# One tiled transformer kernel: the bias row, the causal convolution and the order of cuts around the recurrent block moved between engines

## The reference

```
u = h @ w_in + b_in ;  x_br = u[:, :1024] ;  y_br = gelu(u[:, 1024:])
xc = conv_b + sum over tap of x_br shifted by tap * conv_w[tap]      (4 taps)
r, ig = sigmoid(xc @ w_ga + b_ga), sigmoid(xc @ w_gx + b_gx)         (8 blocks of 128)
a = exp(-8 r softplus(-a_param)) ;  b = sqrt(1 - a*a) * ig * xc
hs = scan of h_t = a_t h_(t-1) + b_t ;  out = (hs * y_br) @ w_o + b_o
gla: b = cumsum of log_sigmoid(...) in chunks of 64 ; q, k scaled by exp(+-b)
```

## Time and profile before

| | us |
|---|---|
| median of 3 runs | 992.35 |
| lowest and highest | 992.27, 993.11 |
| the profiled execution: its time | 992.27 |
| the profiled execution: span from first to last instruction | 991.0 |
| VectorE busy | 680.2 |
| ScalarE busy | 583.2 |
| GpSimd busy | 73.1 |

### The profile page before, as it was taken

The page is one execution under the profiler, slowest core; times in us unless marked ns, Lnnn a source line. Parts: engine busy times, 40 slices in busy tenths (PEclk is TensorE's granted clock), DMA queues, the critical chain, the costliest instruction groups (busy, mean ns, idle before and its releaser), DMA issues.

```text
span 991.0 us, 13523 instructions
## 1 busy us (share of the span) xinstructions
PE 983.3 (99%) x5222; PEld 836.4 (84%) x5222; DVE 680.2 (69%) x1151; ACT 583.2 (59%) x1016; POOL 73.1 (7%) x84
## 2 busy tenths in 40 slices
PE   9999999999999999999999999999999999999997
PEld 6887788888888998888888888888888888888886
DVE  6877776655667888766566678778576544677564
ACT  6677755444547896645454575557675644575443
POOL 2213110000000250000000000000120001000000
PEclk9999999999999999999999999999999999999999
DMA  9753445564555445555655556455543433335551
GB/s 366 296 198 123 175 170 204 200 205 177 203 180 173 168 170 176 184 194 188 215 185 198 186 197 229 174 196 184 186 152 131 170 128 128 128 128 202 181 191 42
DMA packets 27263, 180.32 MB, mean 182 GB/s; under 512 B 3008, under 2 KB 3904, under 8 KB 6464
## 3 DMA queue, kind: packets, MB, share of 16 engines
q1 hardware_dynamic: 26336, 176.89, 50.2%
q0 software_dynamic: 288, 2.10, 0.5%
q10 hardware_dynamic: 576, 0.47, 0.2%
HBM read 178.40 MB, written 1.05 MB: 181 GB/s over the span
## 4 chain that ended last, share of the span: by engine, by line
PE 92%; DVE 5%; ACT 2%; issue 1%; ACTq 0%; DVEq 0%
PE bank L326 23%; PE bank L281 15%; PE bank L283 15%; PE bank L282 15%; PE bank L334 12%; PE bank L296 1%; DVE lo L1287 1%; ACT L L886 1%; PE bank L451 1%; DVE L L1360 1%; PE bank L568 1%; PE bank L297 1%; DVE L L1424 1%; PE bank L427 1%; PE bank L435 1%
## 5 line engine op out<-in xcount | busy, mean ns | idle before, releaser
L1287 DVE TENSOR_TENSOR lo<-raw,hi 128x1024 fp32r<-128x1024 f32 x318 | 378.7, 1237 | 19.5 <-ACT hi L801 19.5
L801 ACT ACTIVATE hi<-raw 128x1024 fp32r<-128x1024 f32 x318 | 320.2, 1050 | 87.3 <-PE bank L283 86.9
L326 PE MATMUL bank<-X,hi 128*128 128x512 f32 x1080 | 284.3, 396 | 0.0
L326 PEld LDWEIGHTS bank<-X,hi 128*128 128x128 f32 x1080 | 196.9, 189 | 34.7
L334 PEld LDWEIGHTS bank<-X,lo 128*128 128x128 f32 x1080 | 147.3, 190 | 10.8
L334 PE MATMUL bank<-X,lo 128*128 128x256 f32 x1080 | 150.6, 282 | 0.0
L832 ACT ACTIVATE bt<-bank 128x256 f32<-128x256 f32 x143 | 54.2, 380 | 153.5 <-PE bank L326 145.2
L1301 DVE TENSOR_TENSOR zr<-bank,bt 128x256 f32<-128x256 f32 x64 | 27.1, 424 | 108.9 <-ACT bt L832 108.9
L281 PE MATMUL bank<-hi,zh 128*128 128x512 f32 x256 | 100.1, 391 | 0.0
L283 PE MATMUL bank<-hi,zl 128*128 128x512 f32 x256 | 99.9, 390 | 0.0
L282 PE MATMUL bank<-lo,zh 128*128 128x512 f32 x256 | 99.7, 389 | 0.0
(11 more groups left out here) (308 smaller groups left out, 1395.8 us busy)
## 6 DMA issues: line engine op xcount, KB each, us to landing
raw<-in_w SPq DMA_DIRECT2D x64, 1024.0 KB, 4.8
raw<-in_rin SPq DMA_DIRECT2D x8, 1024.0 KB, 4.8
raw<-in_wk SPq DMA_DIRECT2D x4, 1024.0 KB, 9.8
raw<-in_wq SPq DMA_DIRECT2D x4, 1024.0 KB, 8.1
raw<-in_wo SPq DMA_DIRECT2D x4, 1024.0 KB, 4.8
raw<-in_mk SPq DMA_DIRECT2D x4, 1024.0 KB, 4.8
raw<-in_mv SPq DMA_DIRECT2D x4, 1024.0 KB, 4.8
raw<-in_rout SPq DMA_DIRECT2D x4, 1024.0 KB, 4.7
```

Of the source, the lines that this page charges most:

```text
L326: return PE.matmul(bank[b][:, :], wh[:, c:c + P], x[:, k_, :, :].rearrange("p a b -> p (a b)"), start=k_ == 0, stop=k_ == NC - 1, skip_gro ...
L801: ACTE.activation(hi[u_ % HIS][:, c], raw[u_ % RAW][:, c], ACT.Copy).then_inc(hi_cut, 1)
L1287: DVE.tensor_tensor(lo[u_ % RAW][:, c], raw[u_ % RAW][:, c], hi[u_ % HIS][:, c].bitcast(F32), ALU.subtract).then_inc(lo_cut, 1)
```

## The change

Five things are changed. The first tap of the convolution goes from ScalarE to VectorE, as a multiplication and addition of two per-partition scalars, and VectorE finishes one n before it joins the next, each step waiting for the one before. Gates 6 and 7 go behind rin 4. The addition of `bo` to `h` goes from VectorE to GpSimd, where it is one operation, ahead of the `ig` products, together with the scaling of `mk` 2 to 5. On ScalarE the high cuts of mv 1 go behind the Gelu and the copies of rin 6, and `gh` 4 and 5 ahead of those of rout 1; on VectorE scans and products are done in pairs in one call, and the low cuts of mv 1 stand behind the first pair's products. In the gv stage VectorE cuts one tile less ahead.

```diff
@@ TensorE
-        plain("rin", 4, X, (4, 5), (6, 7))
+        plain("rin", 4, X, (4, 5))
+        gates(6)
+        gates(7)
@@ ScalarE
             for n in (2 * i, 2 * i + 1):
                 second("rin", n, func=ACT.Identity, bias=gain("rec_b_in", n))
-            for n in (2 * i, 2 * i + 1):
-                a.wait_ge(*free["rin", n])
-                ACTE.activation(xc[:, n, :], xbr[:, n, 0:S], ACT.Identity, scale=gain("rec_conv_w", n),
-                                bias=gain("rec_conv_b", n)).then_inc(tap_made, 1)
...
-        at_tile("rin", 7)
         a.wait_ge(*free["rin", 11])
         ACTE.activation(yb[:, 0:4, :], yb[:, 0:4, :], ACT.Gelu_apprx_tanh).then_inc(y_made, 1)
...
         to_y(6, ACT.Gelu_apprx_tanh)
+        at_tile("rin", 7)
         gated(0)
         to_y(7, ACT.Gelu_apprx_tanh)
         at_tile("mv", 0)
         gated(2)
+        gated(4)
         at_tile("mv", 1)
         copy_tokens(mv, "mv", 0)
-        gated(4)
-        at_tile("rout", 0)
         gated(6)
-        for i in range(1, 4):
+        for i in range(4):
             at_tile("rout", i)
@@ VectorE
-                d.wait_ge(bo_added, 2)
+                d.wait_ge(bo_added, 1)
...
                 joined(xbr[:, n, 3:XW], "rin", n)
-            for w in range(1, 4):
-                for n in (2 * i, 2 * i + 1):
-                    if w == 1:
-                        d.wait_ge(tap_made, n + 1)
-                        d.wait_ge(*free["rin", n])
-                    else:
-                        d.wait_ge(v_step, steps[0] - (0 if w == 3 and n % 2 else 1))
+                d.wait_ge(*free["rin", n])
+                step(DVE.tensor_scalar(xc[:, n, :], xbr[:, n, 0:S], gain("rec_conv_w", n), gain("rec_conv_b", n), ALU.mult, ALU.add))
+                for w in range(1, 4):
+                    own()
                     x = DVE.scalar_tensor_tensor(...)
...
-        lo_to(2 * (T_OF["rin", 5] + HIS))
-        d.wait_ge(bo_in, 16)
-        for s_ in range(2):
-            DVE.tensor_tensor(h[:, s_, :], h[:, s_, :], bo[:, :], ALU.add).then_inc(bo_added, 1)
         lo_to(2 * (T_OF["rin", 6] + HIS))
...
         lo_to(2 * (T_OF["rin", 7] + 2))
-        first = recur(0)
+        recur(0)                       # scans and, now inside it, products
         lo_to(2 * (T_OF["rin", 7] + HIS))
-        gate_y(0, first)
-        gate_y(2, recur(2))
         gated_low(0)
+        recur(2)
         lo_to(2 * (T_OF["mv", 0] + HIS))
         gated_low(2)
-        gate_y(4, recur(4))
+        recur(4)
         lo_to(2 * (T_OF["mv", 1] + HIS))
         gated_low(4)
-        gate_y(6, recur(6))
-        lo_to(2 * (T_OF["rout", 0] + HIS))
+        recur(6)
         gated_low(6)
...
         for i in range(4):
-            lo_to(2 * (T_OF["gv", i] + HIS))
+            at_tile("gv", i)
             decay_sum(i)
             if i:
                 decayed(i - 1)
-        lo_to(2 * (T_OF["dz", 0] + HIS))
+        at_tile("dz", 0)
         decayed(3)
@@ GpSimd
         for j in range(2):
             by_rows(mk, "mk", j, "mem", 2, mk_scaled)
+        g.wait_ge(bo_in, 16)
+        g.wait_ge(hn_made, 4)
+        g.wait_ge(ssq_made, 8)
+        POOL.tensor_tensor(h[:, :, :], h[:, :, :], bo[:, :].unsqueeze(1).to_broadcast([P, 2, D]), ALU.add).then_inc(bo_added, 1)
+        for j in range(2, 6):
+            by_rows(mk, "mk", j, "mem", 2, mk_scaled)
         for n in range(NC):
             g.wait_ge(*free["gate", n, 1])
             POOL.tensor_tensor(ig[:, n, :], ig[:, n, :], xc[:, n, :], ALU.mult).then_inc(gi_made, 1)
-        for j in range(2, 6):
-            by_rows(mk, "mk", j, "mem", 2, mk_scaled)
```

More of the change, by code:

```diff
@@ L117, in build @@
     z_made, z_high, z_low = sem("z_made"), sem("z_high"), sem("z_low")
-    tap_made, xc_made, t_made = sem("tap_made"), sem("xc_made"), sem("t_made")
+    xc_made, t_made = sem("xc_made"), sem("t_made")
     gi_made, a_made, aa_made, mass_made, root_made, drive_made = (
@@ L299, in feature, with plain @@
             return PE.matmul(bank[b][:, :], wh[:, c:c + P], both_, start=False, stop=True, skip_group_check=True)
-        def plain(name, i, x, banks, within=()):
+        def plain(name, i, x, banks):
             t = T_OF[name, i]
@@ L308, in plain @@
                     c = k_ * 256 + j * 128
-                    if j == 1 and k_ == 4:
-                        for n in within:
-                            gates(n)
                     p.wait_ge(lo_cut, cut_at(t, k_ // 4))
@@ L1500, in to_x @@
                         step(x)
-                    else:
-                        x.then_inc(xc_made, 1)
+                x.then_inc(xc_made, 1)
         for i in range(4):
@@ L1522, in recur @@
                 step(DVE.tensor_tensor_scan(tt[:, n, :], rg[:, n, :], ig[:, n, :], 0.0, ALU.mult, ALU.add))
-            return steps[0]
-        def gate_y(n0, scanned):
             for n in (n0, n0 + 1):
-                d.wait_ge(v_step, scanned - 1 + n - n0)
+                d.wait_ge(v_step, steps[0] - 1 + n - n0)
                 if n < 4:
```

## The result

The changed kernel took 997.86 us (median of 6 runs, 996.91 to 998.25) against 992.34 us (6 runs, 992.20 to 993.57): ratio 1.0051, 95% interval 1.0038 to 1.0063. It is slower, as forecast, and lies inside the range of 994.3 to 998.8; the forecast was 996.7. The profiled execution took 997.31 us, with a span of 996.0. Run again beside the experiments, the same kernel took 997.11 us against 992.56 (ratio 1.0045, 1.0031 to 1.0058).

What follows compares the result with a forecast made beforehand. TensorE, busy 983.3 of 991.0 us, was taken as the bound, so only waits caused count: 1.2 + 0 + 2.55 + 0.6 = 4.35 us, 992.3 + 4.4 = 996.7 us, range 994.3 to 998.8.

Steps and rivals of the forecast that it cites:

- main case: Whole kernel: stalls at rin 0, mv 1 to rout 2 and gv 3, none in the convolution; 996.7 us, chance 0.48.
- rival A: Convolution: VectorE becomes the bound, making the third pair and rin 4's cut late; middle 6.0 us, 998.3 us, chance 0.20.
- No stall to win back: Changed stretches: TensorE is busy throughout, so savings on another engine are worth nothing and each wait caused is added.
- The addition on GpSimd: Rin 0: one 4.55 us operation starts 0.17 us before a low cut and holds it; second half late, +1.2 us.
- Rival B: Rin 0: addition runs behind the cut at 308.82, or a long operation releases the port; +3.2 us, 995.5, chance 0.17.
- The convolution: Rin stretch: VectorE's serial order with the added scalings stays in time, cost 0, with 0.4 to 1.0 us of room.
- From the gates to the output rows: Mv 1 +0.95 and +0.25, rout 1 +0.45, rout 2 +0.9 from late cuts; together +2.55 us.
- gv 3: Gv stage: first half's cut ends at 682.97 while TensorE wants it at 682.40, +0.6 us.
- the signs: TensorE waits naming L1287 six or seven times: about 1.2 us at 318, four between 373 and 393, one near gv 3.
- Rival C: At 308.8 and mv 1's cuts: low cuts pass GpSimd each time; +0.8 to +2.1 us, 993.8 us, chance 0.13.
- the rule quoted in the prediction: Shared SBUF port of VectorE and GpSimd: whoever issues first holds it for the whole instruction and the other fully blocks.

Runs made afterwards that it cites:

- moved_serial: Kernel before plus first tap on VectorE in serial order and bo added on GpSimd in eight pieces, other order kept: 993.25 us against 992.70, ratio 1.0007.

## Why the prediction was right

- **The total** came out 1.2 us above the 996.7: the median of 997.86 lies in the stated range but above the 995.9 to 997.6 given for the main case alone, nearer to rival A's 998.3. The traces tell the two apart, not the total: A's wait in the convolution did not occur, and the steps are those of the main case.
- **No stall to win back** held: the steps are flat between the stalls, and no relief of ScalarE (1008 instructions instead of 1016) or VectorE shows anywhere.
- **The addition on GpSimd**: 4.58 us measured, 4.55 forecast; the order of the two starts, 0.12 us apart, as forecast 0.17; the second half's cut the one waited for; 1.28 for 1.2. Rival B (the addition behind the cut, or a long operation that lets go in between) did not occur in any of the four profiles that have it in one piece.
- **The convolution** cost 0 as forecast, with rin 4's first matmul at its old distance. The walk had the four pairs end at 326.9, 334.6, 341.9 and 349.2; they end at 327.2, 334.9, 342.3 and 349.6 in a trace that is 0.3 late from its start, so each within 0.1. The scaling takes 0.41 us where I took 0.35 of 0.35 to 0.48. Where the gates stand inside rin 4, the serial order costs 0.64, as the two runs with that order show; expected there was 0.2, and for moved_serial 0.2 to 0.6.
- **From the gates to the output rows**: 2.67 measured for 2.55, and stall by stall within 0.15. The late order is shown alone, the gates with the convolution, and the meeting of gates and late order at mv 1 too. That within the late order it is the high cuts behind `gh` is read from the traces (VectorE's waits for them) and not shown by a run of its own.
- **gv 3**: 0.76 for 0.6.
- **Where the 0.35 to the trace's 4.7 is**: I priced each stall by the lateness of the cut. Each restart costs TensorE about 0.1 more, which the prediction put at nothing: the matmul after the first takes 0.31 to 0.34 us to start instead of 0.23 (375.02 to 375.36). Five such restarts (at rin 0, mv 1, rout 1, rout 2 and gv 3; where a tile stops twice, the second wait takes up what the first restart cost) are about 0.45. The latenesses by themselves sum to 4.2, a little under the 4.35, so two small errors partly cancel.
- **The rest to the measured 5.5 us** (997.86 less 992.34) is most likely not of the change: the second set of runs has 4.55 for the same kernel, the interval of the first (1.0038 to 1.0063) is 3.8 to 6.3 us, and in the profiled pair 0.3 arose before 8 us.
- Of the signs, one long wait at 318 and one at gv 3 came as named, but the list shows three waits between 373 and 393 instead of four: the fourth (376.69, second half of mv 1) has no bracket and is seen only against the trace of before. The six names of L1281 come out right only with the old one at 87 us.
- Rival C had the cuts passing GpSimd; at mv 1 the two cuts took 3.23 instead of 2.35, held about as forecast.

## What to carry to other kernels

When one engine is busy throughout, price an edit to the others only by walking each in-order queue to the item that the busy engine waits for next; the busy share says nothing, and in this kernel a move of work was free as long as it brought no such item late, be it by the order of a queue or by one long operation. Keep items that feed the bound engine ahead of those that wait for somebody (the high cuts behind `gh` here, by the traces), and hand GpSimd short operations where VectorE works beside it. Two edits that each just use up the slack on one chain can cost more together than the sum of both alone (2.67 us against 2.05 here).

## What was not expected of the hardware

A run's start varies by as much as most effects here, and nearly all of it before 8 us. The first matmul on loaded data begins at 6.46 us in the profile of before, at 7.67 in that of the split addition:

```profile
6.46 0.80 PE L366 MATMUL bank<-hi,X 128*128 128x512 f32 x1
```
```profile
7.67 0.79 PE L363 MATMUL bank<-hi,X 128*128 128x512 f32 x1
```

Over the eleven other profiles the shift at 8 us lies between -0.3 and +1.2 us, whatever the kernel, while behind it an unchanged stretch repeats to 0.08 us over some 300 us. What in the first loads varies was not looked into. So a shift of 0.8 us that eleven timed runs could not tell from nothing (the gv stage) is plain in one pair of traces laid beside each other by matmul.

One row was new in size: GpSimd held VectorE's two-input operation until the end of its own operation of 2048 columns (4.58 us, so that the cut took 4.3 longer), and with eight pieces VectorE got its turn in between (0.5 and 0.2 longer). The trace thus agrees with the rule quoted in the prediction (the Trainium skill, SBUF — State Buffer, Who interferes with whom). It also agrees, within 0.1 us, with the 4.50 us that the Trainium skill gives for such an addition (GPSIMD Engine Reference, section 3.1). In eight pieces the same addition took 8.57 us: five pieces took 0.73 to 0.74 each, and three, each held by a cut, 1.72.
